# A two-layer conv and pooling trunk on 8 cores: channel LayerNorm statistics reduced to one row and spread back

## What is computed

```python
def layer_norm(x, g, b):
    mu = jnp.mean(xf, axis=-1, keepdims=True)
    xc = xf - mu
    var = jnp.mean(xc * xc, axis=-1, keepdims=True)
    return xc * lax.rsqrt(var + LN_EPS) * g + b

def hybrid_layer(x, w_in, ...):
    h = jnp.einsum("btd,de->bte", x, w_in)                 # (B, T, 4608)
    y_a = a_bg * conv3(a_cg * a_v) * silu(a_z)             # mixer A
    u_b = causal_depthwise_conv(b_v * sigmoid(b_g), ...)   # mixer B, 31 taps
    y_b = silu(layer_norm(u_b, ln_b_g, ln_b_b)) * silu(b_z)
    p = multiscale_causal_pool(c_u)                        # mixer C
    y_c = (einsum(p, pool_w) + pool_b) * pool_scale * silu(c_z)
    out = concatenate([y_a, y_b, y_c]) @ w_out
    return layer_norm(DEEPNORM_ALPHA * x + out, ln_g, ln_b)
```

## Time and profile before

| | us |
|---|---|
| median of 3 runs (786.78 to 787.03) | 786.88 |
| the profiled execution | 786.45 |
| its span, slowest core (cores 783.5 to 784.9) | 784.9 |
| TensorE busy | 768.3 (98%) |
| VectorE busy | 490.1 (62%) |
| ScalarE busy | 380.9 (49%) |
| GpSimd busy | 303.7 (39%) |

### The profile page before, as it was taken

One profiled execution on the slowest core, in us unless ns is written; L12 is line 12 of the kernel. 1 busy time (PEld: TensorE's weight loads), 2 busy tenths in 40 slices (PEclk: granted clock), 3 DMA queues, 4 the chain that ended last, 5 costly groups with the idle time before them and its releaser, 6 DMA issues.

```text
span 784.9 us, 16367 instructions; the slowest of 8 cores (783.5 to 784.9 us)
## 1 busy us (share of the span) xinstructions
PE 768.3 (98%) x5269; PEld 411.8 (52%) x5269; DVE 490.1 (62%) x769; ACT 380.9 (49%) x631; POOL 303.7 (39%) x379
## 2 busy tenths in 40 slices
PE   8999999999999999999999999999999999999994
PEld 7566666654444444445555566666444444444441
DVE  1322369967556678556565657986755647976467
ACT  1223467565445575344554477546433457535421
POOL 4120159673101146346111016956501114862393
PEclk9999999999999999999999999999999999999998
DMA  8997799976789874644897896994656677460022
GB/s 121 163 164 155 171 179 154 167 120 165 178 208 208 172 132 60 98 68 80 170 182 175 179 222 110 159 166 70 131 141 179 159 162 192 58 95 1 1 103 112
DMA packets 77058, 108.58 MB, mean 138 GB/s; under 512 B 24496, under 2 KB 46000, under 8 KB 76464
## 3 DMA queue, kind: packets, MB, share of 16 engines
q0 software_dynamic: 28944, 61.22, 46.9%
q1 hardware_dynamic: 48032, 46.31, 23.2%
HBM read 116.78 MB, written 16.78 MB: 170 GB/s over the span
## 4 chain that ended last, share of the span: by engine, by line
PE 94%; DMA 2%; DVE 1%; issue 1%; POOL 1%; DVEq 0%; POOLq 0%
PE ps L556 63%; PE ps L1162 20%; PE ps L716 7%; DMA xT<-xint 2%; PE ps L766 1%; PE ps L975 1%; PE ps L780 1%; DVE xT L593 1%; PE ps L537 0%; POOL wrg L497 0%; PE ps L1085 0%; POOL xT L507 0%; DVE stt L1176 0%; POOL mem L588 0%; DVE mem L593 0%
## 5 line engine op out<-in xcount | busy, mean ns | idle before, releaser
L556 PE MATMUL ps<-xT,wrg 128*128 128x384 bf16 (+6 forms) x2816 | 518.4, 339 | 0.4 <-DMA xT<-xint 0.2
L556 PEld LDWEIGHTS ps<-xT,wrg 128*128 128x128 bf16 x2816 | 273.7, 98 | 227.0 <-issue 7.6
L584 ACT ACTIVATE mem<-ps 128x512 f32<-128x512 f32 (+10 forms) x284 | 132.7, 485 | 179.9 <-PE ps L556 140.7
L1162 PE MATMUL ps<-wo,yb 128*128 128x512 bf16 x768 | 178.8, 379 | 0.0
L588 POOL TENSOR_TENSOR yb<-mem 128x512 bf16<-128x512 f32 (+3 forms) x120 | 126.5, 1060 | 121.0 <-ACT mem L584 60.7
L497 POOL DMA_DIRECT2D wrg<-w_in_r x144 | 80.1, 559 | 212.8 <-PE ps L556 124.9
L1162 PEld LDWEIGHTS ps<-wo,yb 128*128 128x128 bf16 x768 | 75.0, 98 | 86.2 <-issue 0.7
L584 ACT ACT_TABLE_LOAD x72 | 92.4, 1283 | 57.3 <-DVE mv L1200 41.7
L584 ACT ACTIVATE mem<-mem,par 128x512 f32<-128x512 f32 (+3 forms) x80 | 57.7, 729 | 70.6 <-DVE mem L588 60.0
L593 DVE SCALAR_TENSOR_TENSOR Rb<-Rb,ps 128x512 f32<-128x512 f32 (+1 forms) x59 | 40.1, 680 | 64.7 <-PE ps L1162 64.4
L593 DVE SCALAR_TENSOR_TENSOR mem<-mem,par 128x384 f32<-128x384 f32 (+3 forms) x80 | 64.9, 812 | 12.2 <-ACT mem L584 8.0
(11 more groups left out here) (70 smaller groups left out, 366.4 us busy)
## 6 DMA issues: line engine op xcount, KB each, us to landing
wrg<-w_in_r POOLq DMA_DIRECT2D x144, 256.0 KB, 6.0
mem<-mem SPq DMA_DIRECT2D x64, 135.0 KB, 4.1
Rb<-xin SPq DMA_DIRECT2D x16, 512.0 KB, 5.8
x1s<-Rb POOLq DMA_DIRECT2D x16, 512.0 KB, 4.8
Rb<-x1s SPq DMA_DIRECT2D x13, 512.0 KB, 5.5
mem<-mem SPq DMA_DIRECT2D x64, 103.0 KB, 5.1
wo<-w_out_r POOLq DMA_DIRECT2D x24, 256.0 KB, 9.1
out<-Rb POOLq DMA_DIRECT2D x8, 512.0 KB, 3.6
```

The costliest lines, as they stand in the source:

```text
L556: o = P.add("pe", lambda e, kk=kk: e.matmul(bk.ap[:, 0:N], lhsT=wrg_t[:, s, kk, :], rhs=xT(kk, tok0, N), start=(kk == 0), stop=(kk == 7)), ...
L584: return P.add("act", lambda e: e.activation(out=out, in_=in_, func=func, **kw), reads=reads, writes=writes, cost=cost).fin
L1162: o = P.add("pe", lambda e: e.matmul(Po.ap[0:n, :], lhsT=yb_t[:, ec, off:off + n], rhs=wo_t[:, ec, h * 512:(h + 1) * 512], start=(idx == 0 ...
```

## The change

In `lnb` both sums now go into one PSUM bank: the array is used as four column groups of 32, two of them for the channels (groups 0+2 and 1+3 in two rounds) and two for the squares, eight matmuls in all. ScalarE copies the bank out; four DMAs fetch one row of each part and lay it on N/4 partitions of 4 tokens (`tiny`). VectorE and ScalarE work out mean and reciprocal root there, ten small steps on VectorE and one on ScalarE. VectorE splits both into three bfloat16 parts (`tinyb`), six DMAs write them as rows of one, two or three partitions, and two matmuls of three rows by 128 columns of ones spread and add them; two copies on ScalarE bring them back to SBUF. All four squares have buffers of their own. The gate starts at the end of those copies, 1 us of planner time later than before. In unit 3 the last product of phase C runs on VectorE, and the first chunk of the last output projection does its two last steps after both halves' others.

```diff
+            sqb = []
+            for g in range(4):
+                sq = yield from take((Z_SQ, Z_SQ + 1024, Z_X + 2048, Z_X + 3072)[g], BF16, N)
...
             Ps = yield from new_bank()
-            Pq = yield from new_bank()
-            for g in range(4):
-                o = P.add("pe", lambda e, g=g: e.matmul(Ps.ap[:, 0:N], lhsT=ones_t[:], rhs=cbs[g].ap, start=(g == 0), stop=(g == 3)),
...
+            for r in range(2):
+                for i, s in enumerate((cbs[2 * r], cbs[2 * r + 1], sqb[2 * r], sqb[2 * r + 1])):
+                    edge = (r, i) in ((0, 0), (1, 3))
+                    o = P.add("pe", lambda e, i=i, s=s, r=r: e.matmul(
+                        Ps.ap[32 * i:32 * i + 32, 0:N], lhsT=ones_t[:, 32 * i:32 * i + 32], rhs=s.ap, start=(r == 0), stop=(r == 1),
+                        tile_position=(0, 32 * i)), ...
+            f = act(m.ap, Ps.ap[:, 0:N], AF.Copy, Ps.res, m.res, scale=1.0 / 512, psum=True)
...
+            for i in range(4):
+                row = m.ap[32 * i:32 * i + 1, 0:N]
+                row = bass.AP(row.tensor, row.offset, [row.ap[0], [k, r], [1, k]])
+                o = P.add("sp", lambda e, i=i, row=row: e.dma_start(out=ty[:, i], in_=row), reads=m.res, writes=Ry, dma=True,
+                          cost=0.4, land=0.3)
+            yield o.fin + 7.0
...
-            f = stt(rs.ap, Pq.ap[:, 0:N], 1.0 / 512, rs.ap, ALU.mult, ALU.subtract, Pq.res + rs.res, rs.res, psum=True)
-            f = act(rs.ap, rs.ap, AF.Sqrt, rs.res + [R_eps], rs.res, bias=eps_t[:, 0:1])
-            f = P.add("dve", lambda e: e.reciprocal(out=rs.ap, in_=rs.ap), reads=rs.res, writes=rs.res, cost=0.1 + 0.0064 * N).fin
...
+            f = act(ty[:, 3], ty[:, 2], AF.Sqrt, Ry + [R_eps], Ry, bias=eps_t[0:r, 0:1])
+            yield f
+            small(lambda e: e.reciprocal(out=ty[:, 1], in_=ty[:, 3]), Ry, Ry)
+            for p in range(3):
+                f = small(lambda e, p=p: e.tensor_copy(out=hb[:, p], in_=ty[:, 0:2]), Ry, Rh)
+                if p < 2:
+                    small(lambda e, p=p: e.tensor_tensor(out=ty[:, 0:2], in0=ty[:, 0:2], in1=hb[:, p], op=ALU.subtract), Ry + Rh, Ry)
+            for p in range(3):
+                for i in range(2):
...
+                    o = P.add("sp", lambda e, p=p, i=i, row=row: e.dma_start(out=row, in_=hb[:, p, i]), reads=Rh, writes=m.res, dma=True,
+                              cost=0.4, land=0.3)
+            yield o.fin + 8.0
+            yield lambda: spare(3)
+            Pr = yield from new_bank()
+            Pm = yield from new_bank()
+            for i, b in ((1, Pr), (0, Pm)):
+                o = P.add("pe", lambda e, i=i, b=b: e.matmul(b.ap[:, 0:N], lhsT=ones_t[0:3, :], rhs=rw[0:3, i * N:i * N + N], start=True, stop=True),
+            act(rs.ap, Pr.ap[:, 0:N], AF.Copy, Pr.res, rs.res, psum=True)
+            f = act(m.ap, Pm.ap[:, 0:N], AF.Copy, Pm.res, m.res, psum=True)
...
-                tt("pool", yb_t[:, 8 + g, off:off + N], q.ap, sC.ap, ALU.mult, q.res + sC.res,
+                tt("dve" if u == 3 and i == 3 else "pool", yb_t[:, 8 + g, off:off + N], q.ap, sC.ap, ALU.mult, q.res + sC.res,
...
+            steps = [(h, idx) for h in range(2) for idx in range(12)]
+            if final and chunks[s - 1][0] != u:
+                steps = [x for x in steps if x[1] < 11] + [(0, 11), (1, 11)]
```

More of the change, by code:

```diff
@@ L374, in build_nc @@
         p2b_t = sb("p2xb", [128, 2, 1024], BF16)
+        ty_t = sb("tiny", [128, 4, 4, 4], F32)
+        hb_t = sb("tinyb", [128, 4, 3, 2, 4], BF16)
         mem_t = sb("mem", [128, Z_END // 4], F32)
@@ L392, in build_nc @@
         R_ps = mk("ps", 8)
+        R_ty, R_hb = mk("ty", 4), mk("hb", 4)
         R_ini = mk("ini", 2)
@@ L758, in lnb @@
             rs = yield from take(Z_RS + off * 4, F32, N)
[L759 to L774, removed]
+            sqb = []
+            for g in range(4):
+                sq = yield from take((Z_SQ, Z_SQ + 1024, Z_X + 2048, Z_X + 3072)[g], BF16, N)
+                f = act(sq.ap, cbs[g].ap, AF.Square, cbs[g].res, sq.res)
+                sqb.append(sq)
             yield f + 1.5
@@ new lines, in lnb @@
+            for sq in sqb:
+                sq.free()
+            yield o.fin
+            f = act(m.ap, Ps.ap[:, 0:N], AF.Copy, Ps.res, m.res, scale=1.0 / 512, psum=True)
+            Ps.free()
+            yield f + 0.3
+            yield lambda: len(ln_free) > 0
+            il = ln_free.pop(0)
+            k = 4
+            r = N // k
+            ty, Ry = ty_t[0:r, il], [R_ty[il]]
+            hb, Rh = hb_t[0:r, il], [R_hb[il]]
+            for i in range(4):
[3 more added lines that the diff above has]
+                          cost=0.4, land=0.3)
@@ new lines, in lnb, with small @@
+            yield o.fin + 7.0
+            def small(fn, reads, writes):
+                return P.add("dve", fn, reads=reads, writes=writes, cost=0.2).fin
+            small(lambda e: e.tensor_tensor(out=ty[:, 0], in0=ty[:, 0], in1=ty[:, 1], op=ALU.add), Ry, Ry)
+            small(lambda e: e.tensor_tensor(out=ty[:, 2], in0=ty[:, 2], in1=ty[:, 3], op=ALU.add), Ry, Ry)
+            small(lambda e: e.tensor_tensor(out=ty[:, 1], in0=ty[:, 0], in1=ty[:, 0], op=ALU.mult), Ry, Ry)
+            f = small(lambda e: e.tensor_tensor(out=ty[:, 2], in0=ty[:, 2], in1=ty[:, 1], op=ALU.subtract), Ry, Ry)
@@ new lines, in lnb @@
+            yield f + 0.3
+            rw = m.ap.bitcast(BF16)
+            for p in range(3):
+                for i in range(2):
+                    row = rw[p:p + 1, i * N:i * N + N]
+                    row = bass.AP(row.tensor, row.offset, [row.ap[0], [k, r], [1, k]])
+                    o = P.add("sp", lambda e, p=p, i=i, row=row: e.dma_start(out=row, in_=hb[:, p, i]), reads=Rh, writes=m.res, dma=True,
+                              cost=0.4, land=0.3)
+            ln_free.append(il)
+            yield o.fin + 8.0
@@ new lines, in lnb @@
+            yield lambda: spare(3)
[3 more added lines that the diff above has]
+                o = P.add("pe", lambda e, i=i, b=b: e.matmul(b.ap[:, 0:N], lhsT=ones_t[0:3, :], rhs=rw[0:3, i * N:i * N + N], start=True, stop=True),
+                          reads=[R_ones] + m.res, writes=b.res, cost=mmc(N))
+            yield o.fin
+            act(rs.ap, Pr.ap[:, 0:N], AF.Copy, Pr.res, rs.res, psum=True)
+            f = act(m.ap, Pm.ap[:, 0:N], AF.Copy, Pm.res, m.res, psum=True)
@@ L801, in lnb @@
+            Pr.free()
+            Pm.free()
             left = [4]
-            t0 = f - 1.0
+            t0 = f
             if u < 3 and t == len(unit_tiles(li, blk)) - 1:
@@ L813, in lnb @@
             m.free()
-        lnb_busy = [False]
+        ln_free = [0, 1, 2, 3]
         begun = [0]
-        def lnb_free():
-            return not lnb_busy[0]
         def gate(u, g, t, off, N, X, rs, sz, left):
@@ L1256, in chain @@
                 tr[0] += 1
-            return [lambda h=h, idx=idx: mm(h, idx) for h in range(2) for idx in range(12)]
+            steps = [(h, idx) for h in range(2) for idx in range(12)]
+            if final and chunks[s - 1][0] != u:
+                steps = [x for x in steps if x[1] < 11] + [(0, 11), (1, 11)]
+            return [lambda h=h, idx=idx: mm(h, idx) for h, idx in steps]
         def spload(dst, src, w, after=()):
```

17 lines of the change are left out of this document (2 added, 15 removed).

## The result

The changed kernel takes **850.79 us** (median of 4, 848.55 to 852.77) against 786.83 before in the same session: ratio 1.0798, 95% interval 1.0779 to 1.0818. The forecast was 813 with 840 as its upper end: the direction was right and the size was not, +64 us for +26. The result lies above the range's upper end, for which the prediction had left a chance of 0.10. The profiled execution took 852.77, its span is 851.2 us, 66.3 more than before.

The account below looks back on a forecast made before the run. The prediction took TensorE as the bound: delays of 12 + 14 + 5 us from serial transfers, less 4.8 of matmul work and 0.2 at the end, made +26 us, 813 us, range 781 to 840 (the forecast's own 795 to 834).

Parts of the forecast that it names:

- TensorE's work: Over ten tiles: 13.9 us of matmuls removed, less 3.5 sums, 2.1 drains and 3.5 spread, net 4.8 us less.
- the tail: End of phase C and last output: the first output chunk waits less for the last channel group, 0.2 us at most.
- The sums' drain: Statistics matmuls in column groups: changing tiling mode drains TensorE, 0.21 us for each of 10 blocks, 2.1 us in all.
- L975 between full matmuls shows no such gap and the rows are nearest: Spread matmuls: three rows of weights cost no mode-change gap; otherwise up to 2.1 us more, net gain 2.7.
- 10 us of LayerNorm and store, is unchanged: After TensorE's end: the closing 10 us of LayerNorm and store stay as before.
- The chain of ten landings: Each tile's four fetches and six returns go in series through SP; late ones stop TensorE, 12 + 14 + 5 us.
- small pieces are slow everywhere: Rival, all units: 8- and 16-byte pieces take 4.8 us a landing even beside a quiet queue, 906 us, chance 0.04.
- unit 0's delay: Unit 0, third spread: reached at 194 us against 182, 12 us late.
- the landing beside a full q0: Phase A of units 0 and 2: a small transfer beside GpSimd's full queue q0 lands in 4.5 us, bounds 2.4 and 8.2.
- the prediction's own upper end: At 8.2 us a landing beside full q0, delays of 21, 23 and 8 us put the kernel at 834.
- time lost, one for one: TensorE, busy 768.3 of 784.9 us: anything that makes it wait lengthens the kernel by the same amount.
- The faster rival: Units 0 and 2: landings within 2.8 us beside q0 leave no delay, 782 us (779.5 to 784.5), chance 0.36.

Follow-up runs that it names:

- Experiment 5: Changed kernel without the ten transfers a tile (statistics never reach the gates) and with the planner's two margins at 0: 784.10 and 784.84 us in two of five runs.
- experiment 12: Kernel before with only the change's last part, unit 3's last products on VectorE and the first output chunk reordered: 787.38 us against 788.63, ratio 0.9984.
- experiment 3: Changed kernel with fetches and returns free of one another and the three table loads ahead of the first fetches: 803.15 us, ratio 1.0195.
- experiment 2: Changed kernel with only the three table loads moved ahead of the first tile's fetches, transfers still in series: 849.26 us, ratio 1.0778.
- experiments 1: Changed kernel with a tile's four fetches free of one another and its six returns likewise, same 100 transfers: about 810.5 us, ratio 1.0294.
- 8: Changed kernel with tables ahead and only the fetches free of one another, the six returns still in series: 824.81 us, ratio 1.0460.
- 6: Changed kernel without the twelve output weight loads of unit 2: median 849.99; core spans above clock 0.96 had median 830.7 against 844.5, an estimate of 837 us.
- 7: Changed kernel with two bfloat16 parts instead of three, eight landings in series: median 858.42 us; core spans above clock 0.96 had median 834.0, an estimate of 840.
- experiment 11: Kernel with free transfers, tables ahead, half the output weight loads moved, three returns, smaller margins (795.54 us), now with 128-row spread and GpSimd clearing: 802.82 us, ratio 1.0185.

## Why the prediction was right and wrong

**TensorE's work: the total right within 1 us, in part by luck.** I had 4.8 us less, and 5.0 with the tail. Experiment 5 shows the whole of it: a span 2.4 less with 1.6 us more waits than before (7.5 against 5.9 by the lists), so 4.0. Two errors nearly cancel in it, the gap at the spread and the end of the kernel. The sums' drain of 0.21 us a block was right. The choice that "L975 between full matmuls shows no such gap and the rows are nearest" for the spread was wrong: L975 has 128 rows, the spread three, and it pays 2.1 us in ten blocks. I had named that end, 2.7 us for the change without the tail. The tail went the other way: TensorE's 0.2 us came as forecast, but "10 us of LayerNorm and store, is unchanged" was wrong by 1.0 us (experiment 12). With 2.7, 0.2 and 1.0 the sum is 3.9 for the 4.0 measured.

**The chain of ten landings: right, and it is most of the loss.** Without it, experiment 3 against 2, 46 us go; experiments 1 and 8 take it apart and 6 shows that the full queue makes it. Rival "small pieces are slow everywhere" is out: a quiet link is 1.9 us, quicker than the 2.4 I took from the shuffles. The Trainium skill, "DMA: Bandwidth & Descriptors", Specifications, has pieces under 512 bytes written by read-modify-write; if that happens here it costs nothing that the 8-byte pieces, at 1.8 us to landing on a quiet queue, would show.

**The step that failed is the size of unit 0's delay, and first in it the landing beside a full q0.** The prediction took "4.5, a little under the 5.2 of the burst, since no others go beside it"; it measured 6.9 as the mean of eight links in unit 0, and in unit 2 the slow ones between 527 and 567 us took 6.9 to 8.2. The row that was nearest was the earlier trace rows: q0 at 101.8% and 8.2 us, against 98.0% and 5.2 in the earlier trace rows; phase A stood at 105.3%. With 6.9 the same sum makes unit 0 20 us late where I had 12 and unit 2 22 where I had 14, and the kernel some 829. That isn't enough: even the 8.2 of the prediction's own upper end gives 834, 17 us short of the result. So the sum itself lacked something. Unit by unit, TensorE's waits in the traces are 30 us in unit 0 (forecast 12), 2 in unit 1 (0), 18 in unit 2 (14), 7 in unit 3 (5). Units 1 to 3 are near the forecast; that unit 2's 18 is under the 22 that 6.9 us would give is luck, since I have no reason for it. Unit 0 is 18 us off, and 8 of them are the landing by that sum. For the rest, I let the full stretch end at 150 us, while a late TensorE also drags phase A and its loads on, and the links at 147 to 165 us were the slowest, 7.6 and 10.4 us. This dragging follows from the timeline; no run tests it alone.

**Two terms stood at nothing.** First, the clock. Behind long waits TensorE worked at 1.2 GHz: the same matmuls are busy for 774.5 us here, with 52 of 5289 records missing, and for 765.3 in experiment 5, so at least 9 us. Of the span's 66.3 us, 58.8 are waits (the lists add up to 64.7 and 5.9), work and tail are 4.0 less, and 11.5 remain for it. The prediction said of a wait that it is "time lost, one for one"; here a us of wait cost about 1.2. Of the 40 us between forecast and result, waits beyond the forecast's 31 are thus 28, the clock 11.5 and the work 1. Second, the table behind the fetches with VectorE waiting in order. I had counted its landing as a delay of the chain (3.3 us) and not asked who waits for the table. By itself it changed nothing (experiment 2), in a kernel without the chain it is worth 7 us.

**The faster rival** (782 us, 0.36) had a fair price for its case, 784 by experiment 5. Its condition, landings of 2.8 us or less beside q0, isn't met: they are 6.9. Even with the series gone the kernel stands at 795 to 811.

**What stays open.** Why 795 us can't come down to 784 I have only argued: with transfers and margins the gates start late and VectorE's and ScalarE's work piles up in phase C. No run separates that from the banks that the spread takes. Why a small transfer waits so long beside a full queue is open too. And experiments 6 and 7 rest on core spans, not on times.

## What to carry to other kernels

Count a chain of dependent transfers by its links, and price a link by the fullest stretch that it must cross: two DMAs that write disjoint parts of one buffer need a resource each, and that alone was worth 40 us here. When a wait is put in front of a queue, look at everything behind it on that queue and at who waits for it, the small tables too. A wait that the trace shows isn't worth its length while another chain sets the time: moving the table cured the 9.0 us one and gave 1.5 us, but 7 once the chain was gone. And add the waits up as wall time only after a look at the granted clock behind them: here each us of wait cost 1.2.

## What I had not expected of the hardware

A DMA of 0.5 to 2 KB in pieces of 8 or 16 bytes, in series on SP's queue, has a period of 1.7 to 2.2 us in quiet stretches and 5.0 to 10.4 beside GpSimd's full one, though its own queue then takes 1 to 6% of the engines. The Trainium skill, "DMA: Bandwidth & Descriptors", Anatomy of one DMA — SWDGE (gpsimd) path, gives a DMA of GpSimd's queue some 2.0 us of fixed cost; these DMAs are SP's, and the quiet links of this trace are near that figure, the ones beside the full queue aren't. Two matmuls with three rows of weights between full ones cost 0.2 us beyond their columns (experiment 5), and the same two with 128 rows 0.03 (experiment 11). After waits of 9.0 and 13.7 us the granted clock stood at 0.50, and the low clock cost some 10 us in all.
